# Weight sums of a Winograd-style product made by accumulating DMAs from GpSimd instead of VectorE additions

## The reference, cut to what matters

```python
x = x + 0.5 * swiglu(rmsnorm(x), w1_gate, w1_up, w1_down)     # D_FF = 5632
proj = rmsnorm(x) @ w_in                                      # attention and pooling, then @ w_out
x = x + concat(attn, pooled) @ w_out
x = x + 0.5 * swiglu(rmsnorm(x), w2_gate, w2_up, w2_down)
return rmsnorm(x)
def swiglu(h, w_gate, w_up, w_down):
    return (silu(h @ w_gate) * (h @ w_up)) @ w_down
```

## Time and profile before

| | us |
|---|---|
| median of 3 runs | 1722.46 |
| lowest, highest | 1720.77, 2141.56 |
| the profiled execution | 1721.32 |
| its span in the profile | 1719.5 |
| PE busy, DVE busy, ACT busy, POOL busy | 1706.5, 1226.1, 845.6, 204.8 |
| HBM read | 331.71 MB |

### The profile page before, as it was taken

The page is one execution under the profiler, slowest core; times in us unless marked ns, Lnnn a source line. Parts: engine busy times, 40 slices in busy tenths (PEclk is TensorE's granted clock), DMA queues, the critical chain, the costliest instruction groups (busy, mean ns, idle before and its releaser), DMA issues.

```text
span 1719.5 us, 20848 instructions
## 1 busy us (share of the span) xinstructions
PE 1706.5 (99%) x7638; PEld 1414.8 (82%) x7638; DVE 1226.1 (71%) x1417; ACT 845.6 (49%) x989; POOL 204.8 (12%) x376
## 2 busy tenths in 40 slices
PE   9999999999999999999999999999999999999998
PEld 7788888888888888888888888888887888888886
DVE  7988888886555566587877888888888865554554
ACT  6555555554444444454554555555555554443443
POOL 0111111111110000000040001111111111100000
PEclk9999999999999999999999999999999999999999
DMA  8666666666665555665544565666666666655552
GB/s 293 190 215 216 213 214 217 213 209 209 207 208 196 196 195 191 209 202 192 170 153 164 196 196 179 216 214 214 213 217 197 216 220 203 232 190 193 193 195 98
DMA packets 186226, 346.28 MB, mean 201 GB/s; under 512 B 11768, under 2 KB 23984, under 8 KB 186032
## 3 DMA queue, kind: packets, MB, share of 16 engines
q1 hardware_dynamic: 172960, 332.51, 58.7%
q0 software_dynamic: 11264, 11.56, 2.4%
q10 hardware_dynamic: 1936, 1.32, 0.3%
HBM read 331.71 MB, written 2.10 MB: 194 GB/s over the span
## 4 chain that ended last, share of the span: by engine, by line
PE 96%; DVE 1%; issue 1%; ACT 1%; DMA 1%; POOL 0%; ACTq 0%; SPq 0%; DVEq 0%
PE banks L508 28%; PE banks L509 27%; PE banks L510 27%; PE banks L611 3%; PE banks L612 3%; PE banks L610 3%; PE banks L494 2%; PE banks L527 1%; PE banks L497 1%; POOL turned L1805 0%; DMA turned<-squared 0%; PE banks L704 0%; DVE w_lo L1412 0%; PE banks L728 0%; DVE w_lo L1181 0%
## 5 line engine op out<-in xcount | busy, mean ns | idle before, releaser
L1181 DVE TENSOR_TENSOR w_lo<-raw,w_hi 128x1024 fp32r<-128x1024 f32 x366 | 449.7, 1232 | 349.9 <-ACT w_hi L852 348.4
L852 ACT ACTIVATE w_hi<-raw 128x1024 fp32r<-128x1024 f32 x366 | 386.6, 1060 | 513.4 <-PE banks L510 487.6
L508 PE MATMUL banks<-w_hi,act 128*128 128x512 f32 x1280 | 499.1, 390 | 3.2 <-DVE w_lo L1412 3.2
L510 PE MATMUL banks<-w_lo,act 128*128 128x512 f32 x1280 | 498.0, 389 | 0.0
L509 PE MATMUL banks<-w_hi,act 128*128 128x512 f32 x1280 | 498.0, 389 | 0.0
L1412 DVE TENSOR_TENSOR w_lo<-raw,w_hi 128x1024 fp32r<-128x1024 f32 (+1 forms) x288 | 328.7, 1159 | 111.4 <-ACT w_hi L991 109.0
L991 ACT ACTIVATE w_hi<-raw 128x1024 fp32r<-128x1024 f32 (+1 forms) x288 | 286.9, 1010 | 223.7 <-PE banks L510 200.5
L508 PE MATMUL banks<-w_hi,h 128*128 128x512 f32 x832 | 323.8, 389 | 0.0
L510 PE MATMUL banks<-w_lo,h 128*128 128x512 f32 x832 | 323.7, 389 | 0.0
L509 PE MATMUL banks<-w_hi,h 128*128 128x512 f32 x832 | 323.7, 389 | 0.0
L508 PEld LDWEIGHTS banks<-w_hi,act 128*128 128x128 f32 x1280 | 240.3, 188 | 54.5 <-DVE w_lo L1412 4.4
(11 more groups left out here) (173 smaller groups left out, 1194.3 us busy)
## 6 DMA issues: line engine op xcount, KB each, us to landing
raw<-in_w_down SPq DMA_DIRECT2D x88, 1024.0 KB, 5.0
raw<-in_w_gate SPq DMA_DIRECT2D x84, 1024.0 KB, 5.3
raw<-in_w_up SPq DMA_DIRECT2D x84, 1024.0 KB, 5.5
raw<-in_w_in SPq DMA_DIRECT2D x32, 1024.0 KB, 5.2
raw<-in_w_out SPq DMA_DIRECT2D x16, 1024.0 KB, 5.0
turned<-squared POOLq DMA_DIRECT2D x320, 32.0 KB, 5.6
raw<-in_w_up SPq DMA_DIRECT2D x8, 512.0 KB, 9.2
raw<-in_w_gate SPq DMA_DIRECT2D x7, 512.0 KB, 9.5
```

The costliest lines, as they stand in the source:

```text
L508: pe.matmul(dst, operand[:, k, hi], w_hi[:, s, w], start=k == first, stop=False)
L510: mm = pe.matmul(dst, operand[:, k, hi], w_lo[:, s, w], start=False, stop=k == last)
L852: act_e.activation(w_hi[:, s, :], raw[:, (p // 2) % RAW_SLOTS, off:off + PIECE], ACT.Copy).then_inc(hi_ready, 1)
L1181: dve.tensor_tensor(w_lo[:, s, :], raw[:, (p // 2) % RAW_SLOTS, off:off + PIECE], w_hi[:, s, :].bitcast(F32), ALU.subtract).then_inc(lo_re ...
```

## The change

The four DVE additions of a superblock go, and with them the buffer `sums`. POOL starts four DMAs instead (`fast_sums`, `add_weights`), each of which reads 512 KB of weights from HBM a second time and adds them to what stands in `raw` (`accum_op=ALU.add`). T3 is made in the up chunk (u0 += u1), the other three one after another in the low half of the gate chunk: += u0 gives T1, += u1 gives T2, += g1 gives T4. Each of these three waits until DVE has split the piece that stood there. So the gate slot stays taken until piece 15, and the pieces, the slots and the loads' conditions are put in another order. Each sum has a semaphore of its own. The DVE's transposition moves from piece 11 to piece 6, the folds to 14, 16 and 19. In the first plain superblock after the loop, the load of its third chunk gets one more wait.

```diff
-B11_0, B11_1, B21, T1, T3, B22, T2, T4 = 0, 1, 3, 5, 7, 9, 11, 13
+B11_0, B11_1, B21, T3, T1, B22, T2, T4 = 0, 1, 3, 5, 7, 9, 11, 15
-UP_AT = {14 + n: 4 + 2 * n for n in range(6)}
+UP_AT = {13: 4, 14: 6, 16: 8, 17: 10, 18: 12, 19: 14}
-FAST_SLOTS = (0, 1, 2, 3, 2, 3, 0, 1)
+FAST_SLOTS = (0, 1, 2, 3, 2, 3, 1, 0)
-FAST_FREE = (-6, -4, -2, 0, 5, 9, 12, 12)
+FAST_FREE = (-6, -4, 0, 0, 5, 9, 10, 16)
-FOLD_AT = (15, 16, 17)
-MERGE_AT, PRODUCT_AT, SQUARE_H_AT, SPLIT_FAST_AT = 2, 4, 11, 18
+FOLD_AT = (14, 16, 19)
+MERGE_AT, PRODUCT_AT, SQUARE_H_AT, SPLIT_FAST_AT = 2, 4, 6, 18
...
             def load_gate_up(f, i):
                 first, fi = gate_first(f, i), f["sb"] + i
                 for c in range(8):
+                    if i == FAST_SBS + 1 and c == 2:
+                        sp.wait_ge(lo_ready, first)
...
             def round_fast(turn, first, nth, p, shift):
                 act_e.wait_ge(piece_used, first + p - SPLIT_SLOTS + 1)
                 if p in SUMS:
-                    act_e.wait_ge(summed, 4 * nth + SUMS.index(p) + 1)
+                    act_e.wait_ge(summed[SUMS.index(p)], 16 * (nth + 1))
...
-                    if p == B11_1:
-                        add_sum(nth, T1, turn, shift)
-                        add_sum(nth, T3, turn, shift)
-                    if p == B22:
-                        add_sum(nth, T2, turn, shift)
-                    if p == T2 - 1:
-                        add_sum(nth, T4, turn, shift)
...
+            def add_weights(p, slot, part, i, half):
+                pool.dma_start(raw[:, slot, 0:PIECE].rearrange("p (t n) -> p t n", n=QCOLS),
+                               part[half * 2 * P:(half + 1) * 2 * P, i * QCOLS:(i + 1) * QCOLS]
+                               .rearrange("(t p) n -> p t n", p=P),
+                               accum_op=ALU.add).then_inc(summed[SUMS.index(p)], 16)
+
+            def fast_sums(f, i):
+                first, shift = fast_first(f, i), 0 if i % 2 else 2
+                gate, up = FAST_SLOTS[0] + shift, FAST_SLOTS[1] + shift
+                pool.wait_ge(raw_landed[up], (f["turn"] + 2 * i + 1) * 16)
+                add_weights(T3, up, f["up"], i, 1)
+                pool.wait_ge(lo_ready, first + B11_1 + 1)
+                add_weights(T1, gate, f["up"], i, 0)
+                pool.wait_ge(lo_ready, first + T1 + 1)
+                add_weights(T2, gate, f["up"], i, 1)
+                exchange(f["sb"] + i - 1, turned)
+                pool.wait_ge(lo_ready, first + T2 + 1)
+                add_weights(T4, gate, f["gate"], i, 1)
+
             for f in ffns:
-                for i in range(1, GATE_SBS):
+                for i in range(1, FAST_SBS + 1):
+                    fast_sums(f, i)
+                for i in range(FAST_SBS + 1, GATE_SBS):
                     exchange(f["sb"] + i - 1, turned)
```

More of the change, by code:

```diff
@@ L75 @@
 MID_FIRST = GATE_PIECES + ROW_PIECES
-B11_0, B11_1, B21, T1, T3, B22, T2, T4 = 0, 1, 3, 5, 7, 9, 11, 13
+B11_0, B11_1, B21, T3, T1, B22, T2, T4 = 0, 1, 3, 5, 7, 9, 11, 15
 GATE_AT = {2: 4, 4: 6, 6: 8, 8: 10, 10: 12, 12: 14}
-UP_AT = {14 + n: 4 + 2 * n for n in range(6)}
-SUMS = (T1, T3, T2, T4)
+UP_AT = {13: 4, 14: 6, 16: 8, 17: 10, 18: 12, 19: 14}
+SUMS = (T3, T1, T2, T4)
 S5, S7, S2, S12 = range(4)
 P1_BANK, N5_BANK, N7_BANK, R6_BANK = 4, 5, 6, 7
-FAST_SLOTS = (0, 1, 2, 3, 2, 3, 0, 1)
-FAST_CHUNK = {0: (0, 0), 1: (0, 1), 2: (2, 0), 3: (0, 2), 4: (2, 2), 6: (3, 0), 7: (1, 0), 8: (3, 2),
-              9: (1, 2), 10: (4, 0), 11: (1, 2), 12: (4, 2), 14: (5, 0), 15: (5, 2), 16: (6, 0),
-              17: (6, 2), 18: (7, 0), 19: (7, 2)}
-FAST_FREE = (-6, -4, -2, 0, 5, 9, 12, 12)
+FAST_SLOTS = (0, 1, 2, 3, 2, 3, 1, 0)
+FAST_CHUNK = {0: (0, 0), 1: (0, 1), 2: (2, 0), 3: (0, 2), 4: (2, 2), 5: (1, 0), 6: (3, 0), 7: (0, 0),
+              8: (3, 2), 9: (1, 2), 10: (4, 0), 11: (0, 0), 12: (4, 2), 13: (5, 0), 14: (5, 2),
+              15: (0, 0), 16: (6, 0), 17: (6, 2), 18: (7, 0), 19: (7, 2)}
+FAST_FREE = (-6, -4, 0, 0, 5, 9, 10, 16)
 COPY_P1_AT, ROUND_FAST_AT = 8, 17
-FOLD_AT = (15, 16, 17)
-MERGE_AT, PRODUCT_AT, SQUARE_H_AT, SPLIT_FAST_AT = 2, 4, 11, 18
+FOLD_AT = (14, 16, 19)
+MERGE_AT, PRODUCT_AT, SQUARE_H_AT, SPLIT_FAST_AT = 2, 4, 6, 18
 U0, W0 = 48, 64
@@ L189, in layer_kernel @@
         forms = at("forms", [P, 2, 4, 2, P], F32R, fast_at)
-        sums = at("sums", [P, PIECE], F32, fast_at + 8 * PIECE)
         whole = at("whole", [P, 4, 2, P], F32, fast_at + 8 * PIECE)
@@ L258, in layer_kernel @@
         h_squared = sem("h_squared")
-        summed = sem("summed")
+        summed = [sem(f"summed{p}") for p in SUMS]
         whole_act_ready = sem("whole_act_ready")
@@ L980, in round_fast @@
                 act_e.wait_ge(piece_used, first + p - SPLIT_SLOTS + 1)
+                c = FAST_CHUNK[p][0]
+                slot = (FAST_SLOTS[c] + shift) % RAW_SLOTS
                 if p in SUMS:
-                    act_e.wait_ge(summed, 4 * nth + SUMS.index(p) + 1)
-                if p in (T1, T4):
-                    dst, src = w_hi[:, p % SPLIT_SLOTS, :], sums[:, :]
-                else:
-                    c = FAST_CHUNK[p][0]
-                    slot = (FAST_SLOTS[c] + shift) % RAW_SLOTS
+                    act_e.wait_ge(summed[SUMS.index(p)], 16 * (nth + 1))
+                else:
                     act_e.wait_ge(raw_landed[slot], (turn + (1 if c < 4 else 2)) * 16)
-                    off, size = fast_part(p)
-                    dst, src = w_hi[:, p % SPLIT_SLOTS, 0:size], raw[:, slot, off:off + size]
-                act_e.activation(dst, src, ACT.Copy).then_inc(hi_ready, 1)
+                off, size = fast_part(p)
+                act_e.activation(w_hi[:, p % SPLIT_SLOTS, 0:size], raw[:, slot, off:off + size],
+                                 ACT.Copy).then_inc(hi_ready, 1)
             def copy_p1(first, fi):
@@ L1383, in split_forms @@
                 dve.memset(folds[:, :, :], 0.0).then_inc(folded, 1)
[L1385 to L1401, removed]
             def split_fast(first, p, shift):
@@ L1406, in split_fast @@
                 s = p % SPLIT_SLOTS
[L1407 to L1411, removed]
+                off, size = fast_part(p)
+                src = raw[:, (FAST_SLOTS[FAST_CHUNK[p][0]] + shift) % RAW_SLOTS, off:off + size]
                 dve.tensor_tensor(w_lo[:, s, 0:size], src, w_hi[:, s, 0:size].bitcast(F32),
@@ L1457, in fast_gate_up @@
             def fast_gate_up(f, i, shift):
-                turn, first, fi = f["turn"] + 2 * i, fast_first(f, i), f["sb"] + i
+                first, fi = fast_first(f, i), f["sb"] + i
                 nth = f["fast"] + i - 1
```

## The result

The changed kernel takes 1790.04 us (median of four runs, 1789.6 to 1791.2) against 1721.88 us before (median of four runs, those made beside it included). The ratio is 1.040, 95% interval 1.0382 to 1.0418: 68 us slower. One run before, of 2141.56 us, is left out of the ratio. The forecast was 1729 us.

A forecast was written before the change was run, and what follows sets the result against it. PE was taken as the bound, busy 1706.5 of 1719.5 us. 1721.3 + 1.0 (first loop's start) - 1.4 (exchange) + 8.4 (14 stalls of 0.6) = 1729.3, say 1729 us; range 1717 to 1772.

The forecast's parts named there:

- The term -1.4 for the exchange: Transposition at piece 6 starts the exchange earlier, so ACT's wait that reached PE once goes: gain 1.4 us, once.
- D: Rival: the DMA engines fill up; at 6 us per add they need 51.4 us per superblock, 1869 us; chance 0.03.
- A: The forecast case: ring a little longer than PE's 42.16 us, d + a 5.4 to 7.9, 1721 to 1756 us; chance 0.45.
- the length of the ring: Chain from piece 2 of one fast superblock to the next, via T4, c7, c2: 0.6 us stall on 14 boundaries.
- From c2's landing to the split of piece 7: Ring's first stretch, ACT rounding and DVE splitting up to piece 7: 10.64 us, transposition's 1.14 included.
- From there to T4's add: On POOL, T2's issue then the exchange's 16 DMAs (8.4 us) set T4's start: 9.5 us; piece 11's split already met.
- All three hide: Adds T3, T1 and T2 land before they are wanted if an add stays under about 6 to 8 us.
- a: T4's add from issue to landing: 1.1 POOL, 1.2 fixed, 2.6 data, 4.9 us; upper end 9.9.
- d: POOL's own time for one add: 1.1 us, ends 0.53 and 2.1.
- d + a: POOL's add time plus T4's landing: 6.0 us, ends 3.6 and 12.0; above 5.4 PE waits at each boundary.
- C: Rival: a 512 KB add is slow, d + a over 7.9, same place, slower by more than 2%; chance 0.18.
- The sign given for A: One new PE wait, about 14 times 0.6 us, before piece 2 of each fast superblock from the second on.

The follow-up runs named there:

- the last experiment: Kernel before with one number changed, SQUARE_H_AT 11 to 8 (DVE's transposition behind piece 8): 1719.5 us against 1721.5, ratio 0.9988.

## Why the prediction was wrong

**Right.** PE was the bound, and relief of DVE brought nothing: 72 us less of DVE's time, no gain. (The prediction had 78, from 1.22 us each; back to back an addition occupies DVE for 1.13 us, since the next operation starts before it ends.) The way to lose time was the one that the prediction described, T4 to c7 to the next c2, paid on 14 boundaries. It stands in the chain of the changed kernel link by link, and two links (c2's load, the transposition in DVE's stretch) gave 18 us each when shortened. The term -1.4 for the exchange was right, as the last experiment and the run without adds show. The wait at the start of the first loop grew by 0.9 us (2.69 us instead of 1.82), where the prediction had 1.0; the 1.6 us at the lower clock behind it were not in the prediction. D, full DMA engines, did not happen: 0.85 against the 0.90 forecast for A.

**Wrong: the length of the ring.** From one landing of c2 to the next the prediction had 42.8 us, measured are 46.2. The steps that failed, by its own terms:

- *From c2's landing to the split of piece 7.* The prediction had 2.40 + 8.24 = 10.64, measured 11.68 (101.56 to 113.24). It took the moment of split 7 from a trace in which DVE waited for PE. When c2 is late, DVE does piece 2, `merge`, 3, 4, the product, 5, 6, the transposition and 7 in one stretch without a gap, and its own work is the length. The transposition was counted but on the wrong base.
- *From there to T4's add.* The prediction had 9.5, POOL's queue alone, and took the other condition as met: "is met by then if T2's add landed within some 6 us". Measured are 10.6, and it is the other condition that counts: T2's add took 7.6 us, and its path over piece 11 is 0.3 + 7.6 + 2.7. POOL's queue by itself would have been at 10.0, as the 16 DMAs took 9.0 us instead of 8.4. So T2's landing made 0.6 of the 1.1 us and the exchange 0.5. The prediction did say that a later T2 "joins the same ring", but it gave this no term in the sum and no share of the range. Its limit, "All three hide as long as an add stays under about 6 to 8 us", came from the moment when PE wants each sum; T3 took 9.8, T1 8.0 and T2 7.6 us (medians). Where T2's add did land within 6.2 us, T4's started 9.3 us after it, much as predicted.
- *a.* 6.3 us for T4's add, not 4.9. The data part of 2.6 us of all engines was near (3.0 measured). The fixed part was not: 1.2 us came from the quickest DMA of 32 KB in another stretch, while 128 KB here still took 4.1.
- *d* was 1.2 against 1.1, and with T2's landing as the gate it is no term of its own.

The three terms come to 1.0 + 1.1 + 1.4 = 3.5 us, the others to -0.1 together: from the prediction's 42.8 to 46.2, so 4.1 us over PE's 42.16 where the forecast had 0.6. That is 57 us instead of 8. A ring with nearly no slack passes every error on in full, fourteen times; three terms were each short by a little over a microsecond, and the range had let only one of them (d + a) vary. By the prediction's own formula the measured d + a, 1.2 + 6.3 = 7.5, would have cost 2.1 us per superblock, 29 us: within A. So C's sign and place came true, though not at its condition. The sign given for A, one wait of 0.6 us before piece 2, came as two waits, mostly 0.9 us before piece 0 and 1.7 before piece 2.

**Where the rest of the 69.7 us lies.** Both traces have all 7638 matmuls, so the same matmul can be looked up by its number in each (start in us):

| matmul | before | after | later by |
|---|---|---|---|
| first layer: first of fast superblock 1 | 53.83 | 53.33 | -0.5 |
| first of fast superblock 2 | 98.10 | 100.89 | 2.8 |
| first of the plain superblock behind the loop | 393.22 | 425.71 | 32.5 |
| 30 matmuls on | 400.02 | 434.23 | 34.2 |
| second layer: first of fast superblock 1 | 1045.66 | 1079.88 | 34.2 |
| first of fast superblock 2 | 1087.93 | 1125.38 | 37.5 |
| first of the plain superblock behind the loop | 1384.80 | 1452.76 | 68.0 |
| 30 matmuls on | 1391.60 | 1461.25 | 69.7 |

Nothing is lost outside the fast superblocks and the first pieces behind them. The 14 boundaries have 29.7 + 30.5 = 60.2 us, with two waits of 2.0 us behind the loops among them (PE's third row above). The first superblock of each loop, which the prediction charged with 1.0 us once, has 3.3 and 3.2. The lower clock behind the loops has 1.7 twice. Not tried is whether the exchange behind T4's add, in place of before it, would help; nor which of the loads beside T2's add make it slow.

## What to carry to other kernels

When a change moves work from a busy engine to the DMA queues of a kernel whose bound is elsewhere, look first for the ring: buffer freed, load, split, next buffer freed. Add up the latency of all transfers that depend on each other in it and compare with the bound's time for one turn. A transfer that lands before its own deadline can still be a link of that ring, so check it against the ring, too. Take the times for steps as if every engine in the ring arrived late, since in the kernel before they were waiting for somebody else.

## What the runs showed of the hardware that I had not expected

- An accumulating DMA of 512 KB took 1.2 us of POOL for its issue where a copy took 0.72, 272 packets where a copy had 144, and 3.0 us of the 16 engines where a copy had 1.6. To landing T4's took 6.4 us and the others, which run beside chunk loads, 8.0 us; the copies took 4.8 and 5.5 (medians).
- The issue on POOL had the same 1.2 us for rows of 2 KB and of 512 bytes, and to landing the quarter of the bytes still took 4.1 us.
- The loads of the up chunks became slower with the adds beside them: a median of 9.0 us where it had been 5.5. Transfers beside each other slowed the adds, too: T1's add took 8.0 us, and 5.9 where T3's was left out.
- Six waits of PE of 1.8 to 2.7 us were followed by 3.4 us at the 1.2 GHz level, with a matmul every 0.43 us instead of 0.23. It cost about 1.7 us where PE was the bound and nothing that the superblock's length shows (45.9 us) where PE waited anyway.
